# Seven block products in place of eight for the query and key columns of four projection bodies, with the dilated units' copies on ScalarE

## What is computed

```
h = rms_norm(x, pre_g)
qc, kc, vc, gc, qd, kd, vd, gd = _split(h @ w_in, ODD_IN_WIDTHS)
qc = partial_rope(qc.reshape(b, s, C_GROUPS, C_HEADS, HEAD_DIM), pos)
kc = partial_rope(kc.reshape(b, s, C_GROUPS, C_HEADS, HEAD_DIM), pos)
oc = dilated_mixture_attention(qc, kc, vc.reshape(b, s, C_GROUPS, C_HEADS, HEAD_DIM))
```

## Time and profile before

| | us |
|---|---|
| median of 3 runs | 1217.54 (1216.47 to 1217.96) |
| the profiled execution's own time | 1216.43 |
| its span in the profile | 1214.6 |
| TensorE, weight loads | 1196.7, 1001.0 busy |
| VectorE, ScalarE, GpSimd | 707.6, 562.9, 78.7 busy |
| DMA | 219.90 MB, mean 181 GB/s |

### The profile page before, as it was taken

One profiled execution on the slowest core, in us unless ns is written; L12 is line 12 of the kernel. 1 busy time (PEld: TensorE's weight loads), 2 busy tenths in 40 slices (PEclk: granted clock), 3 DMA queues, 4 the chain that ended last, 5 costly groups with the idle time before them and its releaser, 6 DMA issues.

```text
span 1214.6 us, 15429 instructions
## 1 busy us (share of the span) xinstructions
PE 1196.7 (99%) x5756; PEld 1001.0 (82%) x5756; DVE 707.6 (58%) x848; ACT 562.9 (46%) x734; POOL 78.7 (6%) x129
## 2 busy tenths in 40 slices
PE   7999999999999999999999999999999999999997
PEld 5788888888888888788888888888888888888886
DVE  5375555566664955754545545565656546667554
ACT  5554343454555644564444444444344444445442
POOL 2500000300000000010000000001000001000000
PEclk9999999999999999999999999999999999999999
DMA  9995354544436454455453545454544555334541
GB/s 361 251 305 195 141 188 156 173 144 169 173 138 242 173 208 173 173 201 180 157 190 140 180 163 178 169 186 159 208 142 169 187 193 208 139 139 173 179 168 69
DMA packets 33436, 219.90 MB, mean 181 GB/s; under 512 B 4288, under 2 KB 4416, under 8 KB 7920
## 3 DMA queue, kind: packets, MB, share of 16 engines
q1 hardware_dynamic: 30672, 209.73, 48.1%
q0 software_dynamic: 1856, 7.38, 2.4%
q10 hardware_dynamic: 864, 2.18, 0.5%
HBM read 217.17 MB, written 2.10 MB: 181 GB/s over the span
## 4 chain that ended last, share of the span: by engine, by line
PE 95%; DMA 3%; DVE 1%; ACT 0%; SPq 0%; issue 0%; ACTq 0%; DVEq 0%
PE acc L383 85%; PE bank_x L533 2%; DMA probs<-x_nat 2%; PE bank_x L517 1%; PE bank_y L487 1%; DMA raw<-weights 1%; PE bank_x L463 1%; PE bank_y L463 1%; PE bank_y L481 1%; PE bank_x L529 1%; PE bank_y L502 0%; PE bank_x L502 0%; PE bank_x L420 0%; PE bank_y L420 0%; DVE w_lo L899 0%; ACT w_hi L639 0%
## 5 line engine op out<-in xcount | busy, mean ns | idle before, releaser
L383 PE MATMUL acc<-w_hi,act_hi 128*128 128x512 f32 x1560 | 620.7, 398 | 2.6 <-DVE w_lo L899 2.6
L383 PE MATMUL acc<-w_lo,act_hi 128*128 128x512 f32 x1560 | 609.6, 391 | 0.0
L899 DVE TENSOR_TENSOR w_lo<-raw,w_hi 128x2048 fp32r<-128x2048 f32 x195 | 448.0, 2298 | 209.0 <-ACT w_hi L639 208.8
L639 ACT ACTIVATE w_hi<-raw 128x2048 fp32r<-128x2048 f32 x195 | 373.6, 1916 | 241.2 <-PE acc L383 215.5
L383 PE MATMUL acc<-w_hi,act_lo 128*128 128x512 f32 x1560 | 418.6, 390 | 0.0
L383 PEld LDWEIGHTS acc<-w_hi,act_lo 128*128 128x128 f32 x1560 | 293.2, 188 | 62.5 <-DVE act_lo L908 0.6
L383 PEld LDWEIGHTS acc<-w_hi,act_hi 128*128 128x128 f32 x1560 | 293.6, 188 | 60.1 <-DVE w_lo L899 2.3
L383 PEld LDWEIGHTS acc<-w_lo,act_hi 128*128 128x128 f32 x1560 | 294.0, 188 | 56.5
L646 ACT ACTIVATE unit<-acc,pre_r 128x512 f32<-128x512 f32 x78 | 49.3, 684 | 114.9 <-PE acc L383 114.5
L661 ACT ACTIVATE probs<-scores,negm 128x256 f32<-128x256 f32 (+1 forms) x80 | 36.7, 459 | 127.6 <-DVE negm L986 102.3
L334 POOL TENSOR_TENSOR rope_c<-unit,cst 128x256 f32<-128x256 f32 (+1 forms) x19 | 15.1, 797 | 663.8 <-ACT unit L646 663.7
(11 more groups left out here) (172 smaller groups left out, 619.4 us busy)
## 6 DMA issues: line engine op xcount, KB each, us to landing
raw<-weights SPq DMA_DIRECT2D x195, 1024.0 KB, 4.8
resid<-x_turned SPq DMA_DIRECT2D x8, 256.0 KB, 10.1
mix<-rpb POOLq DMA_DIRECT2D x32, 64.0 KB, 25.2
postg<-post_g POOLq DMA_DIRECT2D x2, 1024.0 KB, 24.1
resid<-x_perm POOLq DMA_DIRECT2D x2, 1024.0 KB, 8.3
out<-resid SPq DMA_DIRECT2D x8, 256.0 KB, 2.5
raw<-weights SPq DMA_DIRECT2D x2, 512.0 KB, 6.0
postg<-x_nat ACTq DMA_DIRECT2D x2, 512.0 KB, 9.6
```

The lines of the kernel that those rows point to most:

```text
L383: m = nc.tensor.matmul(tiles[t][:, :], a[:, kt, t * P:(t + 1) * P], w[:, buf, kk * NB:(kk + 1) * NB], start=(kt == 0 and a is act_hi and w ...
L639: nc.scalar.activation(w_hi[:, at % SPLIT, :], raw[:, at % RAW, :], ACT.Copy).then_inc(S["hi_ready"], 1)
L899: nc.vector.tensor_tensor(w_lo[:, at % SPLIT, :], raw[:, at % RAW, :], w_hi[:, at % SPLIT, :].bitcast(F32), ALU.subtract).then_inc(S["lo_r ...
```

## The change

**Block products.** In the four bodies 3 to 6 (`fast_body`), the query and key columns are one product of two by two blocks: two token tiles by two halves of the 2048 rows (A11, A12 for the first tile, A21, A22 for the second), and those halves by query and by key columns (W11, W21; W12, W22). Instead of eight block products there are seven, of two operations each:

| products (name in `FAST_OPS`) | left factor | weights | PSUM bank |
|---|---|---|---|
| W11, then W21 | A11, A12 | W11, W21 | sum_a |
| P, then W22 | A21-A22; A12+A21-A22-A11 | W11+W12; W22 | sum_c |
| Q, then R, then T | A21-A22-A11; A11-A21; A22 | W11+W12+W22; W12+W22; W11+W12+W22+W21 | sum_b |

An operation is 512 weight rows by 512 columns, for one tile: 12 products of 512 columns. The value columns (V, 4 operations) stay as they were, 24 products each. 18 operations make the body; those of V have two slots, the others one, so that there are 22 slots of 12 products and h runs from 0 to 21. The order of the operations is W11 W11 V V P P W21 W22 W22 Q Q V R R W21 T T V.

**Left factors** are made once, by VectorE and ScalarE, in body 0 of layer 1 (`sums`), with high and low parts, in memory of `resid`, `postg` and `mix`. The residual that lies in `resid` is therefore stored in DRAM (`x_kept`, 2 MB) by GpSimd's queue and read back in body 7. The turned query and key of a G unit and a fifth weight buffer (in two halves) lie in the memory of `qT` and `kT`.

**Weight sums** are made by DMA: GpSimd issues 8 accumulating loads of 1 MB a body (`accum_op`), which add a chunk from DRAM to what lies in a `raw` buffer, once the low part of its former content is made; each signals `added`. SyncE makes 10 plain loads a body.

**Splits** in these bodies are made in halves of 1024 columns (`fast_split`), 16 buffers a body so, and two whole ones for the next body's start; TensorE waits for each half of the high part, and of the low part, apart.

**Combinations.** ScalarE takes sum_a out twice (after W11, and after W21). VectorE makes the other columns by five operations of 512 columns that read sum_b or sum_c. The key is ready in slot 17, the query in slot 20; GpSimd now rotates the key first.

**Copies.** For G units, the copies of turned probabilities and of outputs are made by ScalarE. The loop over G units is written out on all engines, and GpSimd's over layer 1.

```diff
+FAST_OPS = (("W11", 0), ("W11", 1), ("V", 0), ("V", 1), ("P", 0), ("P", 1), ("W21", 0), ("W22", 0), ("W22", 1),
+            ("Q", 0), ("Q", 1), ("V", 2), ("R", 0), ("R", 1), ("W21", 1), ("T", 0), ("T", 1), ("V", 3))
+FAST_RAW = (0, 1, 2, 3, 0, 1, 4, 2, 3, 0, 1, 4, 2, 3, 4, 0, 1, 2)
...
         @block.gpsimd
+                    if u.kind == "G":
+                        op, d = first_op(1, u.body), CHUNK0[1] + BODY * u.body
+
+                        for o, chunk in ((4, 4), (5, 5), (9, 6), (10, 7), (12, 4), (13, 5), (15, 2), (16, 3)):
+                            r = FAST_RAW[o]
+                            before = max(n for n in range(o) if FAST_RAW[n] == r)
+                            pool.wait_ge(S["lo_ready"], op + before + 1)
+                            pool.dma_start(raw[:, r, :], weights[d + chunk], accum_op=ALU.add).then_inc(added[r], 16)
...
         @block.tensor
+                    for half in (0, 1) if part is None else (part,):
+                        kks = (2 * half, 2 * half + 1)
+                        if o >= 2 and half == 0:
+                            pe.wait_ge(S["hi_half"], (FAST_N - 2) * k + o - 1)
+                        else:
+                            pe.wait_ge(S["hi_ready"], op + o + 1)
+                        for kk in kks:
+                            for n in range(2):
+                                for t in (0, 1) if name == "V" else (None,):
+                                    m = nc.tensor.matmul(
+                                        fast_bank(name, t)[:, :], fast_left(name, c, kk, t)[n],
+                                        w_hi[:, buf, kk * NB:(kk + 1) * NB],
...
+                        if o >= 2 and half == 0:
+                            pe.wait_ge(S["lo_half"], (FAST_N - 2) * k + o - 1)
+                        else:
+                            pe.wait_ge(S["lo_ready"], op + o + 1)
...
         @block.scalar
+            def fast_split(u, h):
...
+                for half in (0, 1) if part is None else (part,):
+                    if half == 0:
+                        if FAST_OPS[n][0] in FAST_SUMS:
+                            act.wait_ge(added[FAST_RAW[n]], fast_sums(k, n))
+                        else:
+                            act.wait_ge(landed[FAST_RAW[n]], fast_landings(k, n))
+                    if half == 0 and n >= 3:
+                        act.wait_ge(S["half_used"], FAST_N * k + n - 2)
+                    else:
+                        act.wait_ge(S["chunk_used"], op + n - 2)
...
         @block.vector
+                    if h == 17:
+
+                        dve.wait_ge(S["chunk_used"], op + 14)
+                        dve.wait_ge(S["n5_taken"], k + 1)
+                        nc.vector.scalar_tensor_tensor(c22, sum_b[:, :], minus_r[:, :], c22, ALU.mult, ALU.add).then_inc(
+                            S["proj_ready"], 1)
+                    if h == 20:
+
+                        dve.wait_ge(S["chunk_used"], op + 17)
+                        dve.wait_ge(S["c11_taken"], k + 1)
+                        nc.vector.scalar_tensor_tensor(c21, sum_b[:, :], r[1], c21, ALU.mult, ALU.add).then_inc(
+                            S["proj_ready"], 1)
```

More of the change, by code:

```diff
@@ L161, in build @@
         cst = sb("cst", [P, CONST_N])
+        with nc.sbuf_tensor("sums_postg", [P, 2, KT // 2, P], F32R) as sums_postg:
+            pass
         postg = sb("postg", [P, D_MODEL])
@@ L229, in build @@
         x_new = [sem(f"x_new{t}") for t in range(NT)]
-        landed = [sem(f"landed{i}") for i in range(RAW)]
+        landed = [sem(f"landed{i}") for i in range(RAW + 1)]
+        added = [sem(f"added{i}") for i in range(RAW)]
         bias_in_two = [sem(f"bias_in_two{i}") for i in range(UH)]
@@ L244, in loops @@
                     yield Unit(kind, lay, body, index, 0, mask), body, 0
+                elif kind == "G" or eng is nc.gpsimd and lay == 1:
+                    for i in range(count):
+                        yield Unit(kind, lay, body, index, i, mask), body, i
                 else:
@@ L275, in _, with ring @@
                 load_x(2 * c + 1)
[L276 to L283, removed]
+            def ring(first, rounds, chunk, op):
+                with sp.Fori(first, first + rounds) as n:
+                    src = [sp.snap(n * RAW + r + chunk) for r in range(RAW)]
+                    free = [sp.snap(n * RAW + r + op - RAW + 1) for r in range(RAW)]
+                    for r in range(RAW):
+                        sp.wait_ge(S["lo_ready"], free[r])
+                        sp.dma_start(raw[:, r, :], weights[bass.ds(src[r], 1)].rearrange("a p n -> p (a n)")).then_inc(
+                            landed[r], 16)
@@ new lines, in load @@
+            def load(r, chunk, used):
+                sp.wait_ge(S["lo_ready"], used)
+                if r < RAW:
+                    sp.dma_start(raw[:, r, :], weights[chunk]).then_inc(landed[r], 16)
+                else:
+                    for half in range(2):
+                        sp.dma_start(spare[half], weights[chunk][:, half * 2 * NB:(half + 1) * 2 * NB]).then_inc(
+                            landed[r], 16)
+            ring(1, RING - 1, 0, 0)
+            op, d = first_op(1, FAST0), CHUNK0[1] + BODY * FAST0
@@ L284, in _ @@
+            at = CHUNK0[1] + BODY * (FAST0 + FAST)
+            ring(1, (ALL_CHUNKS - at) // RAW - 1, at, RING_END)
             for t in range(NT):
@@ L350, in _ @@
                     turns = ((0, NB), (1, NB), (2, 2 * HEAD)) if u.kind == "D" else ((0, NB), (1, NB))
+                    if layer == 1 and u.body > FAST0:
+                        turns = ((1, NB), (0, NB)) + turns[2:]
                     for k, (blk, cols) in enumerate(turns):
@@ L787, in _ @@
                 for u, b, i in loops(act, layer):
+                    if u is not None and u.kind == "G":
+                        fast_body(u)
+                        continue
                     for s in range(BODY):
@@ L819, in _ @@
                             pre_squares(layer, s - 3)
+                        if u is None and layer == 1:
+                            sums(s)
                         if u is None and s == 4:
```

305 lines of the change are left out of this document (277 added, 28 removed).

## The result

The changed kernel takes 1225.72 us (median of 4 runs, 1225.5 to 1227.75) against 1217.75 (4 runs, 1216.47 to 1218.84) before: a ratio of 1.007, interval 1.0052 to 1.0087. It is slower by 0.7%, and above the forecast range. Its profiled execution took 1225.88 us with a span of 1224.0; the span before was 1214.6.

A forecast was written before the change was run, and what follows sets the result against it. TensorE was taken as the bound, 95% of the chain of waits. From 1216.4 us, 21.8 for removed products came off and 2.0 for late landings was added: 1196.6, or 1197.7 as median; range 1194 to 1218.

The forecast's parts named there:

- Products removed: TensorE in the four dilated bodies: 264 products in place of 288 each, 21.8 us removed from the chain.
- Rival E: Seven products going to one bank each: 0.032 us more on each of 672 would eat the gain; chance 0.03.
- Splits added: Half splits per body: VectorE busy 58.2 of 66.3 us, ScalarE 47.4; both keep ahead of TensorE, costed at nothing.
- copies on ScalarE: Copies queued behind splits in slots 8, 12, 16 and 20: 2.8 us where the slot gives 2.9; nothing on the path.
- Rival D: VectorE or ScalarE late at body ends or in dense slots: 1206 us; chance 0.10.
- Transfers added: DMA per body: 8 accumulations at 5.0 us and 10 plain loads at 2.48, 64.8 us, just under 66.3.
- rival B: DMA engines just full: accumulations of 5.5 us make a body 68.8 us, total 1206, up to 1216; chance 0.12.
- Late landings: Buffers landing after their deadlines in the dilated bodies: costed at 0.5 us a body, 2.0 us.
- GpSimd's queue: Accumulations behind the unit's two rotations: first one issued some 10 us before its split must be done; nothing on the path.
- once only: Left factors in the layer's first body and the kept residual's 2 MB out and back: covered, zero.
- C: Slower: accumulations keep the DMA engines 5.84 us, a body takes 75.9 us, total 1234; chance 0.18.

## Why the prediction was wrong

- *Products removed, 21.8 us: right.* With plain loads in place of accumulations three of the bodies take 66.3 us, as forecast, and one 67.3, and the kernel 1193.1 against 1217.54 - 21.8 = 1195.7. Rival E is out.
- *Splits added, copies on ScalarE: right.* VectorE is busy for 56.3 us and ScalarE for 43.8 a body (58.2 and 47.4 forecast), and of TensorE's stops only one, of 1.5 us, is owed to VectorE alone. Moving the copies by itself costs and gives nothing. Rival D is out for this change; it shows itself only in the variants in which VectorE adds as well.
- *Transfers added: the price was right, the sum was not.* 5.0 us was taken for an accumulation, and 5.16 measured. Its neighbour was too low: the plain loads were put at 2.48, from GpSimd's loads, because they would run back to back; they cost 2.75. So 64.8 us, just under 66.3, became 68.8, just over. The two slips together are 4.0 us, and the sum had 1.5 to spare. The threshold named in the prediction, 5.3 us for an accumulation, assumed 2.92 for a plain load, a price at which its own 5.0 would already have made 69.2 us a body; with the 2.75 measured it is (71.8 - 27.5) / 8 = 5.5. By the prediction's own count 5.16 would therefore still have left 3 us a body of gain, and even the true sum, 68.8, gives rival B's 1206.
- *Late landings, 0.5 us a body: this is the step that failed.* It took 8.3 us for an accumulation and 4.8 for a plain load from lightly loaded queues, and compared them with deadlines of 12 and 6 us. At a share of 0.9 they were 12.0, at most 20.1, and up to 16.2 for the fifth buffer, which the deadlines did not name: they spoke of buffers 0 to 3. Each late filling stopped ScalarE, whose queue is in order, with the copy of the turned probabilities behind it, and so TensorE, six times in four bodies. In place of 2.0 us the bodies lost 297.9 - 4 x 66.3 = 32.7 us. By the method above the granted clock of the four rows, short by 0.02, 0.05, 0.05 and 0.02, accounts for an estimated 10.4 of them, and idle time for the other 22.3.
- *GpSimd's queue, once only.* The first accumulation of the second body was issued at 794.28 us, within the time forecast, and was to have some 10 us; it took 13.4 to land, and ScalarE waited 3.0 us. Issuing it earlier gained some 2 us, not clear of the intervals, so this is a small part. The work done once costs nothing: outside the four bodies the span is 1.3 us shorter.
- *The clock.* The prediction had no term for it: it was at 9 in every slice before, where TensorE hardly ever stopped.
- *Rivals B and C.* The place was theirs, the DMA engines. C had the sign and the right sort of stop (ScalarE's weight copies waiting for transfers), but its price was too high (5.84 against 5.16 measured), so that its 75.9 us a body came near the measured 74.5 partly by luck. The engines' sum, 68.8, explains 10 of the 32.7 us lost; that it is a floor, reached only if nothing is due at a fixed time, was missing from both.

The rows give the cost of adding directly: 5.16 against 2.75 us for a plain load in the same stretch, 1.88 times, and against 2.85 on the same queue, 1.81 times. The Trainium skill, Collectives: The Full Stack, section The bandwidth ceiling, says of a collective's reducing step that the add needs two source reads and so halves the rate. By that rule an accumulation would take an estimated 2 x 2.85 = 5.7 us; the trace agrees but for a tenth (5.16).

## What to carry to other kernels

A load that accumulates cost the DMA engines nearly two plain loads here and delayed the other queue's transfers meanwhile, so compare the demand of the stage with its length and leave room: here 59 of 66 us cost nothing, 64 cost some 16 us over the four bodies, and 68.8 more than the whole gain. How much room is enough depends on what is due when; a kernel with another order, 60 us of DMA work and more on VectorE had bodies of 72.5 us. Read landing times in a stretch as loaded as the one to come, and list every buffer with its deadline and what stands behind its reader in an in-order queue. Where both operands of a sum are in the chip already, an engine with idle time is the cheaper place for it, until that engine's own queue holds up the one that bounds.

## What the runs showed of the hardware that was not expected

- Two queues did not share the 16 engines evenly: while both had work, from 816.3 to 832.0 us, GpSimd's accumulations had 86.8% and SyncE's plain load 17.6%, and this 1 MB took 15.7 us. In the run with plain loads on both queues the fifth buffer's halves landed in 5.2 us in the median.
- In the second body two stops of TensorE, of 2.18 and 2.40 us, were each followed by a stretch at or near half clock (0.50 from 834.4 to 837.0, 0.63 from 850.6 to 853.0), so that stops of 4.6 us went with a loss of 8.2.
- The same GpSimd operation, 128 x 128, took 2.51 us in one place and 0.46 in its neighbour (791.00 and 790.59 us), the long one beside a split of VectorE's that ran from 790.61 to 793.19 us, and the next accumulation was queued behind it.
- Issuing an accumulating load kept GpSimd for 0.87 us, and issuing the same load without the addition for 0.53.
